# Gathers of a product-key layer: V half fetched apart from U, later, and only for weights that are not zero, in five of eight buffer slots

## The chip, the cores and the metric

The kernel runs on one core of one Trainium2 chip, as one program. The metric is the time of one execution on the device in microseconds. The kernel before took a median of 1542.22 us over the runs shown (1538.51 to 1542.54).

## The reference, cut to what matters

Two transformer blocks on 256 tokens of width 1024 are computed one after the other, all in float32. The change lies in the last layer of the second, a feed-forward layer with product keys (PEER). For each token and each of 8 heads it picks 16 of 16384 experts, which makes 128 experts a token:

```python
idx = jnp.take_along_axis(cand_idx, pos, axis=-1)     # 128 tokens x 8 heads x 16
g = jax.nn.softmax(best, axis=-1)
u = expert_u[idx]
v = expert_v[idx]
act = jax.nn.gelu(jnp.einsum('td,thkd->thk', xt, u))
return jnp.einsum('thk,thkd->td', (g * act).astype(xt.dtype), v)
```

`expert_u` and `expert_v` are tables of 16384 rows of 1024 floats (4 KB a row). The gain in front of the layer is large (`norm2_g_2` is drawn near 1 and multiplied by 44.634), so the dot products `xt . u` are tens in size, of both signs.

## The kernel before, in words

The first block, the attention and the recurrence of the second fill the program up to about 880 us; during it GpSimd also copies the two tables into one in HBM, `expert_uv`, whose rows are U beside V, 8 KB.

The last stage takes the experts in **rows**: row `i = 16 n + k` is the k-th expert of group n for each of 128 tokens (one token a partition). There are 16 groups (2 blocks of 128 tokens x 8 heads), so 256 rows. One row is handled in these steps, each on its own engine, with semaphores between them:

- GpSimd (L583 to L604): an indirect DMA gathers `expert_uv[idx]` into a buffer slot, 128 partitions x 2048 floats. There are 9 slots (`UV`, `SLOTS = 9`), and row i waits until TensorE has weighed row i-9 (`row_used`).
- VectorE (`row_dot`, L2399): the product of the U half with `H2N`, the token's vector in PSUM, summed to `dot`. Behind the dot of row k it issues one piece of the top-k of group n+2 (`top_part`), and at one row of a group the softmax's factor (`probabilities`).
- ScalarE (`weight`, L1611): gelu of the dot (`gel`), times the softmax's probability (`wts`), then a copy of the identity scaled by it (`DIAG`, 128 x 128). Once a group it computes the exponentials (`exp_best`), which needs another function table, loaded before and after.
- TensorE (`weigh`, L1163, and the loop in `weigh_rows`, L1199): the diagonal times the V half is added to the sum of the token block in PSUM, two matmuls of 512 columns. A float32 matmul stands in the trace as two records, so a row is four.

Each engine takes the rows in order. In groups 0 to 4 TensorE also makes two query chunks behind rows 2 and 6 of a group and the scores of a later group behind row 8; ScalarE drains them from PSUM in its own order of rows. Everything is issued in the order that the code is written in; the waits alone decide the times.

## Time and profile before

| | |
|---|---|
| Median of the runs shown | 1542.22 us |
| The profiled execution's own time | 1537.5 us |
| Its span in the trace | 1535.7 us |
| TensorE, VectorE, ScalarE, GpSimd busy | 92%, 75%, 52%, 22% |
| Software DMA queue (GpSimd's) | 432.01 MB, 72.4% of the engines' span |
| Mean of all DMA | 377 GB/s, and 421 to 422 in the last stage |

The span runs from the first to the last instruction in the trace. The shares are means over stages that differ; the last stage, some 640 of the 1536 us, is the one that the change touches, and is read by itself.

### The profile page before, as it was taken

How to read it: one execution, taken by the hardware profiler on the slowest of the kernel's cores; microseconds unless marked ns; L12 is line 12 of the kernel's file. 1: busy time of each engine (PE TensorE's matmuls, PEld its weight loads, DVE VectorE, ACT ScalarE, POOL GpSimd, SP SyncE). 2: the span in 40 equal slices, each digit the busy share in tenths (PEclk: the TensorE clock that was granted, in tenths of full speed). 3: DMA queues.
4: the chain of work that ended last, by engine and by line, in shares of the span. 5: the costliest groups of instructions: out<-in, count | busy, mean ns of one | idle time of the engine just before them, and what ended most of it. 6: DMA issues, size and time to landing. Idle time of an engine off the chain costs nothing.

```text
span 1535.7 us, 23394 instructions
## 1 busy us (share of the span) xinstructions
PE 1408.6 (92%) x7668; PEld 1025.0 (67%) x7668; DVE 1145.8 (75%) x2470; ACT 793.2 (52%) x1804; POOL 343.4 (22%) x445
## 2 busy tenths in 40 slices
PE   9999999999999999999999899999788787778777
PEld 8898899898888999998989864544232332222222
DVE  6667988887769988787897696666666667666644
ACT  6656544456666444476964434444444444444433
POOL 1111011111110111111110133443333333333331
PEclk9999999999999999999999999999999999999999
DMA  9999799999998999999999499999999999999996
GB/s 355 355 333 340 278 407 404 387 393 344 357 335 312 398 393 404 388 373 337 359 337 341 151 412 402 421 422 420 422 421 421 421 422 422 421 422 422 421 422 266
DMA packets 119267, 578.21 MB, mean 377 GB/s; under 512 B 11472, under 2 KB 11616, under 8 KB 85904
## 3 DMA queue, kind: packets, MB, share of 16 engines
q0 software_dynamic: 79584, 432.01, 72.4%
q1 hardware_dynamic: 39168, 142.97, 24.6%
q10 hardware_dynamic: 432, 2.19, 0.4%
q8 instruction: 44, 0.72, 0.2%
q14 instruction: 39, 0.32, 0.1%
HBM read 576.08 MB, written 135.27 MB: 463 GB/s over the span
## 4 chain that ended last, share of the span: by engine, by line
PE 47%; DMA 19%; DVE 7%; ACT 7%; issue 3%; POOL 0%; POOLq 0%; ACTq 0%; DVEq 0%
DMA late<-expert_uv,idx 11%; PE PS L1211 8%; PE PS L1171 8%; PE PS L672 5%; DMA attn<-expert_uv,idx 4%; PE PS L661 3%; PE PS L652 3%; PE PS L657 3%; DMA ada<-w_ada 3%; PE PS L678 2%; PE PS L1134 2%; ACT wrg L1623 2%; PE PS L701 1%; PE PS L803 1%; PE PS L917 1%
## 5 line engine op out<-in xcount | busy, mean ns | idle before, releaser
L1277 ACT ACTIVATE early_splits<-ring 128x1024 fp32r<-128x1024 f32 x166 | 175.3, 1056 | 89.2 <-PE PS L672 72.4
L1698 DVE TENSOR_TENSOR early_splits<-ring,early_splits 128x1024 fp32r<-128x1024 f32 x166 | 202.5, 1221 | 24.3 <-ACT early_splits L1277 23.9
L2403 DVE CUSTOM_DVE_ANT_0 attn<-attn,PS 128x1024 f32<-128x1024 f32 x115 | 140.4, 1221 | 91.4 <-DMA attn<-expert_uv,idx 90.1
L2403 DVE CUSTOM_DVE_ANT_0 late<-late,PS 128x1024 f32<-128x1024 f32 x113 | 138.0, 1221 | 92.1 <-DMA late<-expert_uv,idx 91.0
L1615 ACT ACTIVATE gel<-dot 128x1 f32<-128x1 f32 x256 | 51.1, 200 | 254.8 <-DVE dot L2403 254.6
L599 POOL DMA_INDIRECT attn<-expert_uv,idx x115 | 108.5, 944 | 244.1 <-PE PS L1211 96.5
L1211 PE MATMUL PS<-attn,wrg 128*128 128x512 f32 x256 | 128.7, 633 | 32.2 <-ACT wrg L1623 32.2
L599 POOL DMA_INDIRECT late<-expert_uv,idx x113 | 106.7, 944 | 178.4 <-PE PS L1211 93.3
L1211 PEld LDWEIGHTS PS<-attn,wrg 128*128 128x128 f32 x256 | 45.8, 195 | 113.7 <-ACT wrg L1623 70.6
L1211 PE MATMUL PS<-late,wrg 128*128 128x512 f32 x192 | 95.9, 623 | 26.0 <-ACT wrg L1623 25.9
L1171 PE MATMUL PS<-attn,wrg 128*128 128x512 f32 x204 | 98.3, 611 | 13.7 <-ACT wrg L1623 12.3
L1623 ACT ACTIVATE wrg<-con,wts 128x128 f32<-128x128 f32 x228 | 91.5, 401 | 21.7 <-PE PS L1211 0.8
L917 PE MATMUL PS<-product_split,early_splits 128*128 128x256 f32 x344 | 96.7, 281 | 1.9 <-DVE early_splits L1698 1.9
L921 PE MATMUL PS<-product_split,early_splits 128*128 128x256 f32 x344 | 97.3, 283 | 0.0
L922 PE MATMUL PS<-product_split,early_splits 128*128 128x256 f32 x344 | 97.2, 282 | 0.0
L1277 ACT ACTIVATE late_split<-ring 128x1024 fp32r<-128x1024 f32 x65 | 68.6, 1056 | 45.0 <-PE PS L672 33.2
L1211 PEld LDWEIGHTS PS<-late,wrg 128*128 128x128 f32 x192 | 33.3, 191 | 87.7 <-ACT wrg L1623 58.2
L1698 DVE TENSOR_TENSOR late_split<-ring,late_split 128x1024 fp32r<-128x1024 f32 x65 | 79.2, 1218 | 6.9 <-ACT late_split L1277 6.8
L672 PE MATMUL PS<-attn_split,late_split 128*128 128x512 f32 x320 | 82.0, 397 | 0.9 <-DVE attn_split L1704 0.9
L672 PE MATMUL PS<-attn_split,early_splits 128*128 128x512 f32 x320 | 80.7, 393 | 1.0 <-DVE attn_split L1704 1.0
L1171 PEld LDWEIGHTS PS<-attn,wrg 128*128 128x128 f32 x204 | 36.7, 192 | 66.2 <-issue 66.0
L1619 ACT ACTIVATE wts<-gel,prob 128x1 f32<-128x1 f32 x256 | 75.4, 295 | 9.3
(431 smaller groups left out, 3140.2 us busy)
## 6 DMA issues: line engine op xcount, KB each, us to landing
ring<-wstream SPq DMA_DIRECT2D x258, 512.0 KB, 9.0
expert_uv<-expert_u POOLq DMA_DIRECT2D x64, 1024.0 KB, 13.9
expert_uv<-expert_v POOLq DMA_DIRECT2D x64, 1024.0 KB, 15.6
ada<-w_ada POOLq DMA_DIRECT2D x32, 512.0 KB, 10.2
late<-w_ada POOLq DMA_DIRECT2D x16, 512.0 KB, 13.7
late<-wstream SPq DMA_DIRECT2D x4, 512.0 KB, 8.7
attn<-expert_uv,idx POOLq DMA_INDIRECT x115
late<-expert_uv,idx POOLq DMA_INDIRECT x113
```

The source lines that it names most:

```text
L599: gp.indirect_dma_start(UV[i % SLOTS], None, expert_uv, bass.IndirectOffsetOnAxis(ap=idx[:, n % 3, k:k + 1], axis=0)).then_inc(row_landed[ ...
L672: mm = pe.matmul(PS[:, bank, :].rearrange("p (s t) -> p s t", s=2), hi_of(u)[:, k * P:(k + 1) * P], x[:, :, k, :], start=(k == 0), stop=(k ...
L917: mm = pe.matmul(out_o, whi, FH[:, par, :], start=first and o % 2 == 0, stop=False, skip_group_check=True)
L921: pe.matmul(out_o, wlo, FH[:, par, :], start=False, stop=False, skip_group_check=True)
L922: mm = pe.matmul(out_o, whi, FL[:, par, :], start=False, stop=last, skip_group_check=True)
L1171: mm = pe.matmul(PS[:, 2 * b + g, :], DIAG[i % SLOTS], UV[i % SLOTS][:, D + g * 512:D + (g + 1) * 512], start=n % 8 == 0 and k == 0, stop= ...
L1211: mm = pe.matmul(PS[:, 2 * (first // (8 * EXPK)) + g, :], DIAG[m], UV[m][:, D + g * 512:D + (g + 1) * 512], start=False, stop=False, skip_ ...
L1277: act.activation(hi_of(u), raw(u), ACT.Copy).then_inc(hi_ready, 1)
L1619: act.activation(wts[:, s:s + 1], gel[:, s:s + 1], ACT.Copy, scale=prob[:, n % 2, k:k + 1]).then_inc(w_ready, 1)
L1623: act.activation(DIAG[i % SLOTS], ident, ACT.Copy, scale=wts[:, s:s + 1]).then_inc(diag_ready, 1)
L1698: ve.tensor_tensor(lo_of(u), raw(u), hi_of(u).bitcast(F32), ALU.subtract).then_inc(units_begun, 1)
L2403: ve.tensor_tensor_reduce(row, row, H2N[n // 8], 1.0, 0.0, ALU.mult, ALU.add, dot[:, n % 2, k:k + 1]).then_inc(dot_ready, 1)
```

## The change

- There are 8 slots instead of 9; the one that lay over the constants is gone. `DIAG` lies in `wrg` alone.
- In slots 1, 4 and 7 (`JOINT`) a row is fetched as before, U and V together, and weighed in its turn.
- In slots 0, 2, 3, 5 and 6 a row's U half is gathered from `expert_u`, as soon as the dot of the row eight before it is done. Its V half is gathered from `expert_v` by an instruction of its own, which GpSimd issues behind the U of the row six later (`V_LAG`).
- The index of V (`idx_v`) is made by VectorE in the row's own step (`pick_row`), by two small instructions: where the weight is exactly 0, 2^20 is added to the index. The gather has a bounds check at 16383 that lets such an index pass without a transfer; what the slot held stays there and is weighed by 0.
- ScalarE writes the diagonal of such a row seven steps later, and TensorE weighs it at the position of the row eight later. The last five of them are weighed behind row 255.
- The first wait of `probabilities` is on `w_ready` instead of `diag_ready`. The table `expert_uv` is still made in full.

```diff
-SLOTS = 9
+SLOTS = 8
+JOINT = (1, 4, 7)
+V_LAG = 6
+NO_ROW = float(1 << 20)
...
-                if i >= SLOTS:
-                    gp.wait_ge(row_used, i - SLOTS + 1)
-                gp.indirect_dma_start(UV[i % SLOTS], None, expert_uv,
-                                      bass.IndirectOffsetOnAxis(ap=idx[:, n % 3, k:k + 1], axis=0)
-                                      ).then_inc(row_landed[i % SLOTS], 16)
-
-            for i in range(ROWS):
-                row(i)
+                s = i % SLOTS
+                at = bass.IndirectOffsetOnAxis(ap=idx[:, n % 3, k:k + 1], axis=0)
+                if s in JOINT:
+                    if i >= SLOTS:
+                        gp.wait_ge(row_used, weighed_by[i - SLOTS])
+                    gp.indirect_dma_start(UV[s], None, expert_uv, at).then_inc(row_landed[s], 16)
+                else:
+                    if i >= SLOTS:
+                        gp.wait_ge(dot_ready, i - SLOTS + 1)
+                    gp.indirect_dma_start(UV[s][:, 0:D], None, expert_u, at).then_inc(row_landed[s], 16)
+
+            def row_v(i):
+                s = i % SLOTS
+                if s in JOINT:
+                    return
+                gp.wait_ge(rows_picked, separate(i + 1))
+                if i >= SLOTS:
+                    gp.wait_ge(row_used, weighed_by[i - SLOTS])
+                gp.indirect_dma_start(UV[s][:, D:2 * D], None, expert_v,
+                                      bass.IndirectOffsetOnAxis(ap=idx_v[:, s:s + 1], axis=0),
+                                      bounds_check=NKEYS * NKEYS - 1, oob_is_err=False).then_inc(v_landed[s], 16)
+
+            for i in range(ROWS + V_LAG):
+                if i < ROWS:
+                    row(i)
+                if i >= V_LAG:
+                    row_v(i - V_LAG)
...
             def weigh(i):
-                n, k = i // EXPK, i % EXPK
-                b = n // 8
-                pe.wait_ge(row_landed[i % SLOTS], 16 * (i // SLOTS + 1))
-                pe.wait_ge(diag_ready, i + 1)
+                r = i if joint(i) else i - SLOTS
+                if not 0 <= r < ROWS:
+                    return
+                b = r // (ROWS // 2)
+                pe.wait_ge(v_landed[r % SLOTS], 16 * (r // SLOTS + 1))
+                pe.wait_ge(diag_ready, spread_by[r])
...
                 act.activation(wts[:, s:s + 1], gel[:, s:s + 1], ACT.Copy, scale=prob[:, n % 2, k:k + 1]).then_inc(w_ready, 1)
-                if i >= SLOTS:
-                    act.wait_ge(row_used, i - SLOTS + 1)
-                act.wait_ge(w_ready, i + 1)
-                act.activation(DIAG[i % SLOTS], ident, ACT.Copy, scale=wts[:, s:s + 1]).then_inc(diag_ready, 1)
+                if joint(i):
+                    spread_weight(i)
+                if i + 1 >= SLOTS and not joint(i + 1):
+                    spread_weight(i + 1 - SLOTS)
...
+            def pick_row(i):
+                n, k, s = i // EXPK, i % EXPK, i % SLOTS
+                if s in JOINT:
+                    return
+                ve.wait_ge(w_ready, i + 1)
+                ve.tensor_scalar(no_row[:, s:s + 1], wts[:, s:s + 1], 0.0, NO_ROW, ALU.is_equal,
+                                 ALU.mult).then_inc(tokens_marked, 1)
+                if i >= SLOTS:
+                    ve.wait_ge(v_landed[s], 16 * (i // SLOTS))
+                ve.wait_ge(tokens_marked, separate(i + 1))
+                ve.tensor_tensor(idx_v[:, s:s + 1], no_row[:, s:s + 1], idx[:, n % 3, k:k + 1],
+                                 ALU.add).then_inc(rows_picked, 1)
...
                     if k == (4 if n else 14) and n + 1 < GROUPS:
                         probabilities(n + 1)
+                    pick_row(n * EXPK + k)
```

How the instructions stand on GpSimd late in the stage, before (`attn`, `late` and `con` are the tiles in which the slots lie, `idx` the indices; `x3` is three alike):

```order
L599 DMA attn<-expert_uv,idx 128x2048 [waits row_used] x3
L599 DMA late<-expert_uv,idx 128x2048 [waits row_used] x2
L599 DMA con<-expert_uv,idx 128x2048 [waits row_used]
L599 DMA attn<-expert_uv,idx 128x2048 [waits row_used,idx_ready]
L599 DMA late<-expert_uv,idx 128x2048 [waits row_used] x2
L599 DMA attn<-expert_uv,idx 128x2048 [waits row_used] x3
L599 DMA late<-expert_uv,idx 128x2048 [waits row_used] x2
L599 DMA con<-expert_uv,idx 128x2048 [waits row_used]
```

And now, for about six rows at the same place:

```order
L647 DMA attn<-expert_v,idx_v 128x1024 [waits row_used,rows_picked]
L633 DMA late<-expert_uv,idx 128x2048 [waits row_used]
L637 DMA attn<-expert_u,idx 128x1024 [waits dot_ready]
L647 DMA attn<-expert_v,idx_v 128x1024 [waits row_used,rows_picked]
L633 DMA attn<-expert_uv,idx 128x2048 [waits row_used]
L647 DMA late<-expert_v,idx_v 128x1024 [waits row_used,rows_picked]
L637 DMA attn<-expert_u,idx 128x1024 [waits dot_ready]
L637 DMA late<-expert_u,idx 128x1024 [waits dot_ready]
L647 DMA attn<-expert_v,idx_v 128x1024 [waits row_used,rows_picked]
```

Thirteen gathers stand where eight stood, each V behind the U or the joint gather of a row six later, and waits for VectorE (`rows_picked`, `dot_ready`) stand beside the one for TensorE.

VectorE in a group of the second half, before (`ISA` with `PS` is the dot, the `ISA` behind it reads its result; the rest is the top-k):

```order
L2403 ISA late,dot<-late,PS 128x1024 [waits row_landed4]
L2403 ISA dot 128x1
L2330 MAX best<-SQ 128x8 [waits topk_step]
L2403 ISA con,dot<-con,PS 128x1024 [waits row_landed5]
L2403 ISA dot 128x1
L2333 MATCH_REPLACE SQ<-best,SQ 128x256 [waits topk_step]
L2334 MAX_INDEX pk_i<-best,SQ 128x8
L2403 ISA attn,dot<-attn,PS 128x1024 [waits row_landed6]
```

And now, at the same pieces of the top-k:

```order
L2464 ISA late,dot<-late,PS 128x1024 [waits row_landed6]
L2464 ISA dot 128x1
L2391 MAX best<-SQ 128x8 [waits topk_step]
L2473 TENSOR_SCALAR no_row<-wts 128x1 [waits w_ready]
L2478 TENSOR_TENSOR idx_v<-no_row,idx 128x1 [waits tokens_marked,v_landed6]
L2464 ISA late,dot<-late,PS 128x1024 [waits row_landed7]
L2464 ISA dot 128x1
L2394 MATCH_REPLACE SQ<-best,SQ 128x256 [waits topk_step]
L2395 MAX_INDEX pk_i<-best,SQ 128x8
L2464 ISA attn,dot<-attn,PS 128x1024 [waits row_landed0]
L2464 ISA dot 128x1
L2398 MAX best<-SQ 128x8 [waits topk_step]
```

The two instructions of `pick_row` stand between a separate row's piece of the top-k and the next dot, and the first of them waits for the weight that ScalarE makes from the dot just before.

## Rows read from the trace of the kernel before

**Rows 1.** Page of the profile, its span and the traffic in 40 slices.
```profile
span 1535.7 us, 23394 instructions
...
GB/s 355 355 333 340 278 407 404 387 393 344 357 335 312 398 393 404 388 373 337 359 337 341 151 412 402 421 422 420 422 421 421 421 422 422 421 422 422 421 422 266
```

**Rows 2.** Busy time of each engine in a stretch of the gathers.
```profile
core 0: us, PE busy (x) PEld busy (x) DVE busy (x) ACT busy (x) POOL busy (x), PEclk, DMA share, GB/s
1300.00:1340.00 40.00, 31.46 (x66) 10.96 (x64) 27.49 (x75) 17.26 (x53) 15.03 (x16) 1.00 1.01 422
```

**Rows 3.** Timeline of VectorE: index casts behind rows 79 and 223, last dot.
```profile
1084.76 0.27 DVE L2374 CAST idx<-SQ 128x16 uint32<-128x16 f32 x1
...
1448.66 0.17 DVE L2374 CAST idx<-SQ 128x16 uint32<-128x16 f32 x1
...
1526.95 1.22 DVE L2403 CUSTOM_DVE_ANT_0 late<-late,PS 128x1024 f32<-128x1024 f32 x1 [1.23 <-DMA late<-expert_uv,idx]
```

**Rows 4.** Timeline of TensorE: row matmuls (L1171) and queries (L1134), groups 1 to 4.
```profile
940.31 3.62 PE L1134 MATMUL PS<-XN,MEM 128*128 128x256 f32 x16
...
982.48 5.31 PE L1171 MATMUL PS<-attn,wrg 128*128 128x512 f32 x12
987.63 3.62 PE L1134 MATMUL PS<-XN,ring 128*128 128x256 f32 x16
...
1054.53 3.62 PE L1134 MATMUL PS<-XN,ring 128*128 128x256 f32 x16
```

**Rows 5.** Timeline of one row's turn, all engines: start, length, what.
```profile
1301.45 1.22 DVE L2403 CUSTOM_DVE_ANT_0 late<-late,PS 128x1024 f32<-128x1024 f32 x1 [0.31 <-DMA late<-expert_uv,idx]
...
1302.59 0.08 DVE L2403 DVE_READ_ACCUMULATOR2_ANT dot<- 128x1 f32 x1
...
1302.71 0.20 ACT L1615 ACTIVATE gel<-dot 128x1 f32<-128x1 f32 x1 [1.46 <-DVE dot L2403]
...
1302.95 0.29 ACT L1619 ACTIVATE wts<-gel,prob 128x1 f32<-128x1 f32 x1
...
1303.33 0.40 ACT L1623 ACTIVATE wrg<-con,wts 128x128 f32<-128x128 f32 x1
...
1303.57 0.94 POOL L599 DMA_INDIRECT attn<-expert_uv,idx  x1 [1.55 <-PE PS L1211]
...
1303.79 1.98 PE L1211 MATMUL PS<-late,wrg 128*128 128x512 f32 x4 [0.50 <-ACT wrg L1623]
```

**Rows 6.** Busy time of each engine in a stretch of weight loads and table copies.
```profile
500.00:540.00 40.00, 40.00 (x269) 36.87 (x268) 35.73 (x56) 19.05 (x24) 6.00 (x11) 1.00 1.02 401
```

**Rows 7.** Timeline of GpSimd's first gathers, and the gathers' issues by tile `idx`.
```profile
883.60 0.94 POOL L599 DMA_INDIRECT attn<-expert_uv,idx  x1 [0.30 <-issue]
884.85 0.94 POOL L599 DMA_INDIRECT late<-expert_uv,idx  x1 [0.30 <-issue]
...
L599 POOL DMA_INDIRECT late<-expert_uv,idx x113: 937/939/1267, 879.5 to 1509.3; - x113
```

**Rows 8.** Timeline of VectorE: small instructions with a dot behind them, a top-k piece.
```profile
886.47 0.17 DVE L2371 SCALAR_TENSOR_TENSOR SQ<-SQ 128x8 f32<-128x8 f32 x1
886.67 0.17 DVE L2374 CAST idx<-SQ 128x8 uint32<-128x8 f32 x1
886.75 1.21 DVE L2403 CUSTOM_DVE_ANT_0 attn<-attn,PS 128x1024 f32<-128x1024 f32 x1
...
937.95 0.29 DVE L2396 TENSOR_SCALAR prob<-gexp 128x16 f32<-128x16 f32 x1
938.33 1.22 DVE L2403 CUSTOM_DVE_ANT_0 late<-late,PS 128x1024 f32<-128x1024 f32 x1
...
1365.70 0.68 DVE L2367 TENSOR_REDUCE SQ<-SQ 128x32 f32<-128x512 f32 x1
```

**Rows 9.** Timeline of ScalarE: first table load of a softmax to the next gelu.
```profile
1318.67 1.28 ACT L1608 ACT_TABLE_LOAD   x1
...
1321.67 0.20 ACT L1615 ACTIVATE gel<-dot 128x1 f32<-128x1 f32 x1
```

More of the change, by code:

```diff
@@ L389, in two_blocks @@
         row_landed = [sem(f"row_landed{k}") for k in range(SLOTS)]
+        v_landed = [row_landed[k] if k in JOINT else sem(f"v_landed{k}") for k in range(SLOTS)]
+        tokens_marked, rows_picked = sem("tokens_marked"), sem("rows_picked")
         h2_ready = sem("h2_ready")
@@ L467, in halves, with separate, joint, orders @@
             return PS[:, bank, :].rearrange("p (s t) -> p s t", s=2)[:, :, 0:nk]
+        def separate(rows):
+            return rows // SLOTS * (SLOTS - len(JOINT)) + sum(k not in JOINT for k in range(rows % SLOTS))
+        def joint(i):
+            return i % SLOTS in JOINT
+        def orders():
+            weighed, spread = {}, {}
+            for i in range(ROWS + SLOTS):
+                r = i if joint(i) else i - SLOTS
+                if 0 <= r < ROWS:
+                    weighed[r] = len(weighed) + 1
+                for r in (i, i + 1 - SLOTS):
+                    if 0 <= r < ROWS and joint(r) == (r == i):
+                        spread[r] = len(spread) + 1
+            return weighed, spread
+        weighed_by, spread_by = orders()
+        first_weighed = [min(range(b * ROWS // 2, (b + 1) * ROWS // 2), key=weighed_by.get) for b in range(2)]
+        last_weighed = [max(range(b * ROWS // 2, (b + 1) * ROWS // 2), key=weighed_by.get) for b in range(2)]
         block = ctx.enter_context(nc.Block())
@@ L1226, in _ @@
             natural_h2(1)
-            weigh_rows(6 * EXPK, 8 * EXPK - 1)
-            weigh(8 * EXPK - 1)
+            weigh_rows(6 * EXPK, 8 * EXPK - SLOTS)
+            for i in range(8 * EXPK - SLOTS, 8 * EXPK):
+                weigh(i)
             for k in range(EXPK):
@@ L1242, in _ @@
                     mm.then_inc(tile_for["act"], handed(4 + g, "act"))
-            weigh_rows(9 * EXPK, ROWS - 1)
-            weigh(ROWS - 1)
+            weigh_rows(9 * EXPK, ROWS - SLOTS)
+            for i in range(ROWS - SLOTS, ROWS + SLOTS):
+                weigh(i)
         @block.scalar
@@ L1666, in _ @@
                         exp_best(n + 2)
+            for i in range(ROWS + 1 - SLOTS, ROWS):
+                if not joint(i):
+                    spread_weight(i)
         @block.vector
```

43 lines of the change are left out of this document (23 added, 20 removed).

## The prediction

> **What bounds the kernel now.** First the stretches. In the last stage (row gathers, from about 890 us to the end) the DMA engines are busy without a gap and move 422 GB/s, while VectorE works 27.5 of 40 us, TensorE 31.5, ScalarE 17.3 and GpSimd 15.0 [rows 1, 2]. A gather of 128 rows of 8 KB is 1.0486 MB, so at 422 GB/s one takes 2.485 us, and that is the pace: the index casts of groups 4 and 13, nine groups of 16 rows apart, start 363.9 us apart, 2.527 us a row; from the dot of row 79 (1083.6, its cast less 1.15) to the last dot, at 1526.95, it is 443.3 us for 176 rows, 2.52 a row [rows 3]. The stage is bound by bytes. Groups 1 to 4 are different: there TensorE also makes queries and scores. Four records of one row take 1.72 us back to back (twelve in 5.15), a query 3.6, the scores about 1 [rows 4], so a group needs 16 x 1.72 + 7.2 + 1 = 35.8 us of TensorE; the queries at 940.31 and 1054.53, three groups apart, show 38.1 a group, against 39.8 for the bytes (16 x 2.485). Bytes and TensorE are almost level there.
>
> Then one turn, from the timeline [rows 5]. Times from the start of the dot: result read 1.14, gelu 1.26, weight 1.50 to 1.79, diagonal 1.88, matmul 2.34 to 4.32. VectorE does its piece of the next top-k behind the read.
>
> **What goes.** In slots 0, 2, 3, 5, 6 the V half of a row is fetched only where the weight is not zero. The trace cannot say how many are. The reference, evaluated on the inputs it draws, can: the dots have a standard deviation of about 46, gelu is exactly 0 below about -5, and 54.0% of the weights of these slots are nonzero. In half-rows of 4 KB per partition a round of eight rows costs 3 x 2 + 5 x 1.54 = 13.7 instead of 16 (half of them are V). Pace of the bytes: 13.7/16 x 2.485 = 2.13 us. Three additions. The groups with a top-k run 0.04 slower than the bytes alone (2.527 against 2.485), kept: 2.17. The skipped partitions fall unevenly on the sixteen DMA engines; if each serves eight partitions, whichever they are, the fullest has over a token block some 1.5% more than the mean by the reference's weights: 2.20. And 4 KB pieces may be dearer than 8 KB ones: a stretch that streams and copies 4 KB rows with the engines equally full moved 401 GB/s [rows 6]. That 5% on the 56% of bytes that are now in 4 KB pieces would make 2.26. Bounds of the byte pace: 2.13 and 2.26.
>
> **What is added on GpSimd.** 160 gathers: 13 issues in a round for 8. An issue takes 0.94 and the next follows 1.25 after it when nothing holds it [rows 7]; a half row is as many pieces (128) as a whole one, so I take the same price: 13/8 x 1.25 = 2.03 us a row. It hides behind the bytes, with 0.17 us to spare. The bounds check and the skipping are in no row. Bounds: 0.94 and 1.27, the longest of the gathers' issues in the trace [rows 7]; with 1.27 + 0.31 all through it is 2.57 a row, above the pace of before. I take 1.25, since the median is 0.939 and the minimum 0.937. Queued behind V of row i-6 is U of row i+1. V of row r waits for its index (about 2.2 after the start of dot r) and for TensorE to have passed position r (about 4 after it, by the chain of rows 5 and one more turn of 1.7); U of r+7 is wanted 7 turns, 15 us, after dot r, so about 10 us of transfers stay queued. The gather queue should not run dry.
>
> A rule of the Trainium skill speaks against this part. The row first: with VectorE at work in most of every window the issue stayed at a median of 0.939, and one was 1.27 [rows 2, 7]. The skill's page "SBUF — State Buffer", section "Who interferes with whom", says that GpSimd shares an SBUF port pair with VectorE, and that certain copies and tensor-scalar forms of VectorE shut GpSimd out while it writes descriptors. By the median the 160 added gathers cost nothing; by the rule, with the new small VectorE instructions, they could each come nearer 1.27. This is rival C.
>
> **What is added on VectorE.** 320 small instructions, two in a separate row's own turn, the first behind the row's weight. Nothing may start past them, the next dot above all. The weight ends 1.79 after the dot's start; I let the first start at 1.85. A dependent small instruction follows 0.20 behind its forerunner and a dot 0.08 behind that; in another place the dot came 0.38 after a small instruction [rows 8]. The pair costs between 0.28 and 0.76 (twice 0.38). I take 0.35, nearer the low end because there the dot had landed and nothing else stood between. A separate turn is then at least 2.20, in which the top-k piece is hidden unless it is longer than 0.7. A joint turn stays at VectorE's own work: 27.49 us for 16 rows [rows 2], 1.72, with gaps 1.87. A group: 8 x 2.20; one of 2.45, where the piece of 0.68 and what follows it is the longer arm [rows 8]; one of 2.86 behind the softmax, since its two table loads hold ScalarE for 3.0 us [rows 9] and row 12, a joint one, absorbs all but 0.65; and 6 x 1.87. Sum 34.1, or 2.13 a row. So VectorE comes level with the bytes; with the dear pair (0.76) it is 38.2, 2.39 a row.
>
> **Groups 1 to 4.** Before, VectorE ran ahead with dots while ScalarE stood waiting to drain a query bank. Now the index of a separate row waits for that row's weight, which stands behind the drain, so VectorE is tied to TensorE's position. Walking one group row by row with the durations of [rows 4, 5, 9], TensorE's 35.8 us get 2.5 of waiting for the diagonal of row 12 (late by the table loads) and about 1 for those of rows 15 and 1: 39.2 against 38.1. Three groups: +3 us. The bytes saved here buy nothing.
>
> **The end.** A separate row is weighed at the position of the row eight later, so five rows are left when the last diagonal comes: 5 x 1.72 = 8.6 us more behind the last dot, which before stood 8.75 us ahead of the end of the span [rows 1, 3]. The same five are missing in group 0; there VectorE's top-k pieces hold the row, so I give nothing back. ScalarE's later diagonals are as many as before and hidden: 0.3 each with over 20 us idle in a window of 40.
>
> **The sum.** The dot of row 79 started at 1083.6; now 1086.6. For the 176 rows after it I take 2.22, just above the two paces of 2.20 and 2.13 because a wait of either is not always covered by the other: 390.7. Last dot at 1477.3, end of span 1477.3 + 8.75 + 8.6 = 1494.7, against 1535.7: -41. The profiled execution took 1537.5 (1.8 around its span) and would take 1496.5; the runs shown have a median of 1542.2, 4.7 above it, so the forecast for the median is 1501.
>
> **Rivals.** A is the forecast, rate 2.17 to 2.28: 1492 to 1512. Chance 0.62.
>
> B: the weight's wait on VectorE takes the place of the bytes. With the pair at 0.76, 2.39 a row: 176 x 2.39 = 420.6, end 1524.6, time 1531. It cancels the gain at 2.44 a row, a pair of 0.84. For it: every separate turn now contains a round trip to ScalarE, and the earliest V transfer into the index's slot must have landed too. Against: ScalarE idles over half of each window. Chance 0.12.
>
> C, slower: GpSimd becomes the bound. At 1.58 an issue, 2.57 a row: 452 us, end 1556, time 1562. It decides from 2.44/1.625 = 1.50 an issue, 0.25 above the 1.25 shown. For it: the bounds check is in no row, and one issue did take 1.27; against: the even issue times. Chance 0.08. (The Trainium skill's page "SBUF — State Buffer", cited above, would have the issues drift that way.)
>
> D, slower: the change does not do what it says. If ScalarE's gelu leaves tiny values instead of zeros, or a skipped index still costs its transfer, the bytes are those of before: 2.52 a row, 443.5, end 1547.4, time 1554. Between, each tenth of V rows more adds 0.1 x 5/8 x 1.24 = 0.08 a row, 14 us; the gain is gone near nine tenths. For it: no row shows a weight. Chance 0.08.
>
> F: the early groups gain after all. If TensorE keeps the five rows' start and loses nothing to ScalarE, -8.6 instead of +3, and 2.17 after: end about 1476 to 1478, time 1484. For it: TensorE was nearly level there. Chance 0.10.
>
> **Numbers.** Predicted 1501. Own range of A 1492 to 1512; the range for 8 in 10 takes in F and most of B: 1484 to 1540. A measurement of this kernel can tell about 0.3% (4.6 us) from no change. Faster: A, F and seven of B's twelve, 0.79. Same: 0.05. Slower: C and D, 0.16.
>
> **What would show it.** In the profile after: gathers' bytes lower by 38 MB (160 x 0.46 x 0.524) and the rate still near 420 or VectorE's dots waiting for weights, not data; issues on GpSimd at 0.94; two small VectorE instructions 1.85 behind a dot's start and the next dot at 2.2; casts of groups 4 and 13 some 320 us apart (9 x 35.5) for 363.9; queries of groups 1 to 4 still 38 to 39 apart; five rows of matmuls back to back at the end. An unchanged byte count would prove D; issues of 1.2 and more back to back C; a dot-to-dot time of 2.6 in separate rows B.

## The result: no gain, a little slower

The changed kernel takes 1548.86 us (median of 20 runs, 1542.23 to 1556.38) against 1539.84 for the one before (20 runs, 1537.85 to 1546.22), a ratio of 1.0062 with a 95% interval of 1.0047 to 1.0077. The forecast was 1501, with a chance of 0.79 for faster and a range for 8 in 10 of 1484 to 1540; the measured time lies above it. The profiled execution has a span of 1542.8 us, where the sum of the prediction came to 1494.7.

The page of the changed kernel, with the lines that answer to [rows 1] and those on GpSimd and the packets:

```profile
span 1542.8 us, 24370 instructions
...
PE 1396.0 (90%) x7668; PEld 1040.5 (67%) x7668; DVE 1180.9 (77%) x2790; ACT 777.8 (50%) x1804; POOL 503.3 (33%) x605
...
GB/s 348 348 343 336 272 404 405 396 397 348 355 336 304 399 398 402 377 365 334 348 330 345 146 299 309 355 360 358 350 373 382 371 331 371 374 379 392 375 380 241
DMA packets 142315, 541.46 MB, mean 351 GB/s; under 512 B 23032, under 2 KB 23176, under 8 KB 129424
```

The bytes fell as forecast, from 578.21 to 541.46 MB, by 36.75 (38 were forecast), but with them fell the rate: 350 to 392 GB/s in the slices from about 1000 us on, once 331, where [rows 1] show 422. The line of the kernel before for the packets:

```profile
DMA packets 119267, 578.21 MB, mean 377 GB/s; under 512 B 11472, under 2 KB 11616, under 8 KB 85904
```

Two stretches of the changed kernel by busy time, the first to be laid beside [rows 2]:

```profile
core 0: us, PE busy (x) PEld busy (x) DVE busy (x) ACT busy (x) POOL busy (x), PEclk, DMA share, GB/s
1300.00:1340.00 40.00, 33.17 (x72) 13.74 (x71) 30.34 (x96) 16.60 (x54) 26.22 (x27) 0.96 0.98 374
1100.00:1500.00 400.00, 316.77 (x695) 130.09 (x693) 298.65 (x897) 165.85 (x538) 257.61 (x267) 0.97 0.98 374
```

No engine is full; GpSimd, the one that grew, is busy 26 of 40 us. Nor does the DMA share of 0.98 say that the transfers are: at a full rate they moved 422 GB/s before, and in the run without V gathers, below, the share reads 0.96 at 367. But GpSimd's 267 gathers in 400 us are one in 1.50 us, which becomes the clue below. VectorE's casts behind rows 31, 79 and 223 and its last dot, to be laid beside [rows 3] (the cast behind row 31 in the kernel before comes last):

```profile
977.70 0.17 DVE L2435 CAST idx<-SQ 128x16 uint32<-128x16 f32 x1
...
1101.84 0.17 DVE L2435 CAST idx<-SQ 128x16 uint32<-128x16 f32 x1
...
1450.99 0.35 DVE L2435 CAST idx<-SQ 128x16 uint32<-128x16 f32 x1
...
1525.47 1.22 DVE L2464 CUSTOM_DVE_ANT_0 late<-late,PS 128x1024 f32<-128x1024 f32 x1 [0.73 <-DMA late<-expert_uv,idx]
```

```profile
964.27 0.17 DVE L2374 CAST idx<-SQ 128x16 uint32<-128x16 f32 x1
```

So row 79 is 17.1 us later than before (1101.84 against 1084.76). From the dot of row 79 (1100.69, the cast less 1.15) to the last dot it takes 424.8 us for 176 rows, 2.41 a row: quicker than the 2.52 of before, far from the 2.22 of the forecast. From the last dot to the end of the span it is 17.33 us; the forecast had 17.35. The difference to the forecast sum, 48.1 us, is 34.1 of pace and 14.1 of start (row 79 was put at 1086.6).

### The profile page after: what moved, and what is told of

Its sections match the earlier page's. It is cut to its first block, busy times and chain, and to the rows that moved or that the text cites. A ratio compares the mean times of both kernels' runs of the same rounds, so it can differ in the third digit from the quotient of the medians.

```text
span 1542.8 us, 24370 instructions
## 1 busy us (share of the span) xinstructions
PE 1396.0 (90%) x7668; PEld 1040.5 (67%) x7668; DVE 1180.9 (77%) x2790; ACT 777.8 (50%) x1804; POOL 503.3 (33%) x605
## 2 busy tenths in 40 slices
DMA packets 142315, 541.46 MB, mean 351 GB/s; under 512 B 23032, under 2 KB 23176, under 8 KB 129424
## 3 DMA queue, kind: packets, MB, share of 16 engines
q0 software_dynamic: 102624, 395.19, 70.2%
q10 hardware_dynamic: 432, 2.19, 0.4%
## 4 chain that ended last, share of the span: by engine, by line
PE 50%; DVE 16%; issue 10%; DMA 10%; ACT 8%; POOL 5%; another core or an unknown queue 2%; POOLq 0%; DVEq 0%; ACTq 0%
PE PS L723 6%; DMA ada<-w_ada 6%; PE PS L1225 6%; PE PS L712 4%; PE PS L703 4%; PE PS L708 4%; PE PS L729 3%; PE PS L1262 3%; DVE late L2464 3%; PE PS L854 3%; PE PS L752 2%; DVE attn L2464 2%; DMA attn<-expert_u,idx 2%; DMA late<-expert_uv,idx 2%
## 5 line engine op out<-in xcount | busy, mean ns | idle before, releaser
L1759 DVE TENSOR_TENSOR early_splits<-ring,early_splits 128x1024 fp32r<-128x1024 f32 x166 | 202.4, 1220 | 24.6 <-ACT early_splits L1328 24.2
L1262 PE MATMUL PS<-late,wrg 128*128 128x512 f32 x288 | 145.8, 634 | 57.9 <-issue 37.7
L2464 DVE CUSTOM_DVE_ANT_0 attn<-attn,PS 128x1024 f32<-128x1024 f32 x128 | 155.5, 1216 | 25.8 <-issue 9.2
L2464 DVE CUSTOM_DVE_ANT_0 late<-late,PS 128x1024 f32<-128x1024 f32 x128 | 156.2, 1221 | 23.5 <-issue 14.5
L1225 PE MATMUL PS<-late,wrg 128*128 128x512 f32 x224 | 111.8, 626 | 39.9 <-ACT wrg L1666 34.7
L1262 PEld LDWEIGHTS PS<-late,wrg 128*128 128x128 f32 x288 | 53.6, 194 | 139.8 <-issue 110.6
L647 POOL DMA_INDIRECT attn<-expert_v,idx_v x96 | 96.5, 1005 | 122.6 <-PE PS L1225 38.7
L637 POOL DMA_INDIRECT attn<-expert_u,idx x96 | 90.1, 939 | 104.0 <-DVE idx L2435 74.8
L1262 PEld LDWEIGHTS PS<-attn,wrg 128*128 128x128 f32 x288 | 55.4, 197 | 90.4 <-issue 75.3
L1225 PEld LDWEIGHTS PS<-late,wrg 128*128 128x128 f32 x224 | 42.0, 196 | 96.5 <-issue 96.0
L576 POOL DMA_DIRECT2D expert_uv<-expert_v x49 | 26.9, 549 | 229.5 <-DMA expert_uv<-expert_u 217.4
L2473 DVE TENSOR_SCALAR no_row<-wts 128x1 f32<-128x1 f32 x160 | 24.4, 153 | 96.6 <-ACT wts L1677 54.4
L576 POOL DMA_DIRECT2D expert_uv<-expert_u x49 | 27.0, 550 | 188.9 <-DMA expert_uv<-expert_v 188.0
```

The lines of the kernel that those rows point to most:

```text
L637: gp.indirect_dma_start(UV[s][:, 0:D], None, expert_u, at).then_inc(row_landed[s], 16)
L647: gp.indirect_dma_start(UV[s][:, D:2 * D], None, expert_v, bass.IndirectOffsetOnAxis(ap=idx_v[:, s:s + 1], axis=0), bounds_check=NKEYS * N ...
L1225: mm = pe.matmul(PS[:, 2 * b + g, :], DIAG[:, r % 8, :], UV[r % SLOTS][:, D + g * 512:D + (g + 1) * 512], start=r == first_weighed[b], sto ...
L1262: mm = pe.matmul(PS[:, 2 * (first // (8 * EXPK)) + g, :], DIAG[:, m, :], UV[m][:, D + g * 512:D + (g + 1) * 512], start=False, stop=False, ...
L1759: ve.tensor_tensor(lo_of(u), raw(u), hi_of(u).bitcast(F32), ALU.subtract).then_inc(units_begun, 1)
L2464: ve.tensor_tensor_reduce(row, row, H2N[n // 8], 1.0, 0.0, ALU.mult, ALU.add, dot[:, n % 2, k:k + 1]).then_inc(dot_ready, 1)
```

## The experiments

"Pace" below is always the time from the dot of row 79 to the last dot over 176 rows, in the profiled execution. The kernels of gathers alone and of the small ring, and those with sixteen gathers, with thirteen in the kernel before and with four joint slots and all V skipped, have one execution each. Three theories stood at first: **D**, the transfers (a skipped partition costs time all the same, or 4 KB pieces are dear); **V**, VectorE's wait for the weight; **G**, GpSimd, its order of gathers at first, and from the second round on their number.

**Gathers alone.** A kernel that only gathers, in stretches: 8 KB rows, pairs, and the mix of the changed kernel, thirteen gathers in eight rows, with 46%, none and all of V skipped. Its core:

```
for i in range(80):
    gather 8 KB if i % 8 in JOINT else gather U (4 KB)
    r = i - 6
    if r >= 0 and r % 8 not in JOINT: gather V of r, bounds_check=16383
```

> This kernel computes nothing: it only issues gathers from GpSimd into buffer slots, eight deep and drained between sections, with index tables drawn at random, and writes zeros as output. Sections: (1) 48 gathers of 8 KB rows; (2) 32 pairs of an 8 KB gather and a 4 KB gather; (3) 32 pairs of an 8 KB gather and a bounds-checked 4 KB gather with every index out of bounds; (4) the same with 46% of the indices out of bounds; (5 to 7) ten rounds each of the kernel's own mix of 13 gathers for 8 rows, with 46%, none and all of the V indices out of bounds. Theory D (the transfers: a skipped partition still costs engine time, and a 4 KB piece costs more than half of an 8 KB one): 8 KB gathers 2.49 us apart; the pairs with all skipped at least 0.4 us above that, about 3.1; the mix with 46% skipped about 18.8 us a round (2.35 a row). Theory V or G (the transfers are as cheap as I counted, and the order of waits loses the time): pairs with all skipped no more than 0.1 above an 8 KB gather (or held at two issues, 2.55), the mix 17.0 to 17.4 us a round (2.13 to 2.17 a row).

Rows 32 to 72 of the three mixes came every 2.14 us with 46% skipped, 2.53 with none, 2.06 with all; 8 KB rows alone every 2.49. An 8 KB row beside an all-skipped gather came every 2.55: such a gather costs the transfers at most 0.06. The windows of the mixes with 46%, none and all skipped:

```profile
core 0: us, DVE busy (x) POOL busy (x), PEclk, DMA share, GB/s
...
500.00:640.00 140.00, 0.00 (x0) 103.72 (x108) 1.00 1.02 411
...
700.00:840.00 140.00, 0.00 (x0) 88.23 (x92) 1.00 1.02 414
...
920.00:960.00 40.00, 0.00 (x0) 30.24 (x33) 1.00 0.97 353
```

The transfers keep 411 GB/s, and the changed kernel's 0.898 MB a row would take 2.19 us. D falls, and the forecast's byte pace stands. With all skipped the pace is GpSimd's: 13 issues in 16.46 us, 1.27 each, without a pause.

**All of V read, none of V read.**

```diff
-NO_ROW = float(1 << 20)
+NO_ROW = 0.0                                   # all read
...
-... wts[:, s:s + 1], 0.0, NO_ROW, ALU.is_equal, ALU.mult)
+... wts[:, s:s + 1], 0.0, NO_ROW, ALU.mult, ALU.add)      # all skipped
```

> The changed kernel with 0 instead of 2^20 added to the index where the weight is zero, so that every V row is read. Its output is the same. Bytes as in the kernel before, 13 gathers a round. Theory D with about 0.6 us for a gather that is all skipped: skipping saves 0.625 x 0.46 x (1.28 - 0.6) = 0.2 us a row, so this runs some 35 to 50 us longer than the changed kernel, near 1590. Theory V (VectorE's turn is the bound, the transfers have slack): the pace goes only from 2.41 to the 2.49 of the bytes, +14 to +20 us, near 1565.

> The changed kernel with every V index of the five slots out of bounds: no V row is fetched there, and the matmuls weigh what the slot holds, so the output leaves those rows out. The instructions and waits are the same. Theory D: the transfers fall to about 2.1 us a row, and the pace to VectorE's 2.17: about 35 to 45 us faster than the changed kernel, near 1508. Theory V or G (waits of VectorE on the weight, or GpSimd's order): the pace stays at 2.35 to 2.41, 0 to 12 us faster, 1537 to 1549.

Reading all V (same instructions, the bytes of before): 1574.62 us, ratio 1.0213 (1.0189 to 1.0236), pace 2.57. Reading none of it in the five slots: 1549.02, ratio 1.0042 (1.0020 to 1.0065), pace 2.41, the same as with 46% skipped, at far fewer bytes. Its window:

```profile
1300.00:1340.00 40.00, 33.84 (x73) 14.02 (x73) 31.59 (x98) 17.64 (x58) 25.19 (x26) 0.96 0.85 298
```

So skipping does save 26 us against the same kernel that reads all; but the last bytes saved buy nothing, and the 2.41 isn't set by bytes.

**The index one step later.** In each step VectorE makes the index of the row before, whose weight has long come.

```diff
-                    pick_row(n * EXPK + k)
+                    if n or k:
+                        pick_row(n * EXPK + k - 1)
```

> The changed kernel with the index of V made one step later on VectorE (behind the next row's dot and its top-k piece), so that VectorE need not wait for ScalarE in the row's own turn; the rest as it is. Theory V: the 0.27 us a row that the first small instruction waited, and the 7 us in group 0, come back: 40 to 50 us faster than the changed kernel, near 1500. Theory D: only the start comes back, 5 to 12 us, near 1540.

1535.22 us, ratio 0.9961 (0.9944 to 0.9978). All of the gain lies ahead of row 79: from the first dot to that of row 79 it takes 199.2 us, against 213.5 in the changed kernel and 200.3 before. The pace doesn't fall: 2.44, where the changed kernel has 2.41. V holds for the start and falls for the rest.

**The number of gathers.** Four kernels, with 8, 12, 13 and 16 gathers in eight rows.

```diff
 # the changed kernel without its V gathers (V halves set to zero once)
                 if i >= SLOTS:
                     gp.wait_ge(row_used, weighed_by[i - SLOTS])
-                gp.indirect_dma_start(UV[s][:, D:2 * D], None, expert_v, ...)
...
 # four joint slots, with the later index
-JOINT = (1, 4, 7)
+JOINT = (1, 3, 5, 7)
...
 # the kernel before, with a second gather that moves nothing
                 row(i)
+                gp.indirect_dma_start(scrap[:, 2 * i:2 * i + 2], None, cells, <nowhere>, bounds_check=...)
```

> The changed kernel with the V gathers of the five separate slots left out: GpSimd waits for the index and for TensorE at their places as before, but issues nothing (V halves are set to zero once, and TensorE multiplies those). VectorE makes all indices, ScalarE all weights, in the same order. Eight issues in a round of eight rows instead of thirteen, and bytes of 1.71 us a row at the pace of the gathers alone. G (the number of gathers on GpSimd is the bound, 13 at 1.48 for eight rows = 2.41): the pace after row 79 falls to what VectorE's own walk needs, 2.13 to 2.2 a row, 40 us earlier than the 424.8 for 176 rows. V (round trip of the weight on VectorE): 2.4 a row stays, the span within 8 us of 1543.

> Slots 1, 3, 5 and 7 joint instead of 1, 4 and 7, and the index made one turn later, as in the run with the index one step later (span 1534.8, 2.435 a row after row 79). Twelve gathers in a round instead of thirteen; bytes of a round 4 x 2 + 4 x 1.54 = 14.2 sixteenths of 2.485 x 8, 2.20 a row. G: 12/8 x 1.48 = 2.22 a row, so 176 x 0.21 = 37 us off that run: last dot near 1480, span 1495 to 1500, and the ratio to the kernel before 0.972 to 0.978. V: the wait for the weight is already a turn behind, the pace of 2.43 is then VectorE's and ScalarE's chain, and one separate row less in eight changes it by at most a twentieth: span 1520 to 1535.

> The kernel before, with a second gather behind each of its 256: into 8 bytes of each partition of a spare tile, all indices out of bounds, so that it moves nothing and nobody waits for it. Sixteen issues in a round of eight rows. With an even issue of 1.27 a round takes 20.3 us, 2.53 a row: level with the 2.52 a row that the bytes set, span 1536 to 1545. G with its 1.48 for a gather: 2.96 a row, 110 us more over 256 rows, span near 1640. V expects the first.

> The kernel before with the second, all-skipped gather only behind rows of slots 0, 2, 3, 5 and 6: thirteen gathers in eight rows instead of sixteen (2.88 a row). G: 13/8 x 1.44 to 1.48 = 2.34 to 2.41 a row, less than the 2.52 that the bytes need, so the span stays at 1536 to 1545. If instead a skipped gather costs the transfers time (0.36 us each, by the run with sixteen: 2.88 less 2.52), the cost is added: 2.52 + 0.625 x 0.36 = 2.74 a row, span 1590.

Without V gathers, but with all their waits, indices and weights: pace 2.03, span 1465.3, ratio 0.953 (0.9491 to 0.957). Four joint slots: pace 2.31, 1508.82 us, ratio 0.9792 (0.9759 to 0.9825). Sixteen gathers, the eight more moving nothing and awaited by nobody: pace 2.88, 1640.52 us, 98 more than before. Thirteen of that kind: 2.56, span 1560.0, where the bytes alone want 2.49; neither no change nor the 2.74 of a cost to the transfers, so the two bounds add a little where they are close. Without V gathers VectorE makes every index behind its weight in its own turn, as in the changed kernel (only its and TensorE's waits for V to land are gone), at 2.03 a row: V is out. It also moves the same bytes as the run that reads none of V, which has its thirteen gathers and 2.41. G has it: 16 gathers at 2.88 are 1.44 each, 13 at 2.41 are 1.48.

The windows of the kernel without V gathers and of the one with sixteen:

```profile
1300.00:1340.00 40.00, 35.60 (x81) 14.57 (x80) 35.18 (x115) 19.04 (x63) 18.59 (x20) 1.00 0.96 367
```

```profile
1300.00:1340.00 40.00, 25.09 (x50) 10.59 (x51) 21.73 (x57) 16.12 (x49) 24.22 (x25) 0.83 0.87 325
```

GpSimd reads 24.2 of 40 where it is the bound: its busy time leaves out 0.30 behind each issue, and pauses. (TensorE's granted clock reads 0.83 in that window of the kernel with sixteen, but TensorE is busy only 25.1 of its 40 us.) The gathers of the changed kernel about one such pause, with GpSimd's timeline first, then TensorE's and VectorE's:

```profile
1313.01 1.00 POOL L647 DMA_INDIRECT late<-expert_v,idx_v  x1 [0.30 <-issue]
1314.32 0.94 POOL L637 DMA_INDIRECT attn<-expert_u,idx  x1 [0.31 <-issue]
1315.56 0.94 POOL L637 DMA_INDIRECT late<-expert_u,idx  x1 [0.30 <-issue]
1319.51 1.00 POOL L647 DMA_INDIRECT attn<-expert_v,idx_v  x1 [3.01 <-remote]
1320.81 0.94 POOL L633 DMA_INDIRECT late<-expert_uv,idx  x1 [0.30 <-issue]
...
1313.33 1.88 PE L1262 MATMUL PS<-attn,wrg 128*128 128x512 f32 x4
1315.04 1.88 PE L1262 MATMUL PS<-late,wrg 128*128 128x512 f32 x4
...
1315.72 0.15 DVE L2473 TENSOR_SCALAR no_row<-wts 128x1 f32<-128x1 f32 x1 [0.65 <-issue]
1317.33 0.16 DVE L2478 TENSOR_TENSOR idx_v<-no_row,idx 128x1 uint32<-128x1 f32 x1 [1.45 <-DVE no_row L2473]
```

The gather at 1319.51 is V of row 165. Its index was made at 1313.42, and TensorE's matmuls at that position, the upper of the two rows, ended at 1315.21, by their record; it could have gone at 1316.8. Between the dots of rows 79 and 240 GpSimd spends 57 us in gaps beyond the usual 0.30, 43 of them in 20 pauses for which index, dot and TensorE's matmul had all ended in time by their records. The 57 us are 0.36 a row: 2.06 and 0.36 make the 2.41.

But the wait was not met. The timeline puts the release down to `remote`, a semaphore event that no recorded end matches, and the semaphore events kept in the trace say which: TensorE's count `row_used` was raised at 1318.66 and again at 1318.73, and GpSimd's wait for it ended at 1318.69. The raise for a matmul that ended at 1315.21 came 3.5 us later, in one burst with the next. Of the 20 pauses 17 end so, within 0.03 us behind a raise of TensorE's count, up to 4.7 us after the matmul's end. TensorE's ends are modelled in these traces, so by its rows alone the matmul could have been late. VectorE's rows speak for late signals: its second small instruction follows the first by 0.26 us as a rule, here by 1.61, and it waited for nothing but the first one's own signal; in 5 of 145 turns the dot's result reached an idle ScalarE 0.4 to 2.1 us late, before in none of 152. Raises of TensorE's count more than 0.2 us behind its latest recorded end, between rows 79 and 240 and of those that the trace shows: none of 162 before, 37 of 97 in the changed kernel, 30 of 115 with all V skipped.

**Whose pauses are they?** Four kernels tried to bring them about, on the view that GpSimd's waits were met.

> It computes nothing of the reference. Five stretches of 80 rows, each with the mix of thirteen gathers in eight rows of the changed kernel, V six rows behind; in the first four all indices of V are out of bounds, in the fifth 46%. Beside them VectorE: (1) idle; (2) row dots from PSUM and SBUF, 128 x 1024, back to back; (3) pairs of 128 x 1 instructions of the kind that make the index; (4) a dot, a 128 x 256 product and a pair, in turn; (5) dots, as in 2. In the gathers alone, measured before, such rows came every 2.057 us (13 issues at a mean of 1.266) and 2.14 with 46% skipped. G, GpSimd as the bound by work of its own that VectorE's work makes dearer: in the changed kernel 13 gathers take 19.2 to 19.3 us over many turns, 1.48 each, in runs of even issues with one pause of 3 us; by that (1) is 2.06 and (2) or (4) near 2.4 a row, with such pauses. V, the weight's round trip: nothing here waits for VectorE, so all of 1 to 4 stay at 2.06 and 5 at 2.14. If all five stay, VectorE's port or load is not what makes a gather dearer in the kernel, and the 3 us pauses come from a wait in the kernel's own order.

> It computes nothing of the reference. Five stretches of 80 rows of gathers in the changed kernel's mix, V six rows behind. Alone, and beside VectorE's dots, such rows came every 2.07 us with all V skipped and 2.12 with 46% skipped (1.27 to 1.30 a gather), while inside the kernels a gather costs 1.44 to 1.48 on the average, because GpSimd pauses for 3 to 4 us every 13 to 34 gathers with its waits long met. Here: (1) beside matmuls of TensorE, all skipped; (2) beside ScalarE's 128 x 128 copies; (3) beside both and VectorE's dots; (4) as the kernels do it: no gather waits for a landing, each waits for the dot that freed its slot, V for its own row's dot, and VectorE waits for the landings; (5) as 4 with 46% skipped. If the pauses come from the load of another engine, 1, 2 or 3 goes to 2.3 to 2.4 a row with pauses of 3 us; if they come from the way in which gathers wait (a dot instead of a landing), 4 does; if from neither, all stay at 2.07 and 5 at 2.12 to 2.2, and the cause of the pauses stays open.

> It computes nothing of the reference. Four stretches of 80 rows of 8 KB gathers, each row waiting for the dot (1) or for TensorE's two matmuls (2 to 4) of the row eight earlier, VectorE's dot behind each landing; beside each row a second gather whose indices are all out of bounds (in 4 only in five rows of eight; in 3 of 8 bytes a partition and without any wait, as in the run where the kernel before has such a gather behind each of its own, 2.88 a row). Alone, such pairs came every 2.54 us, which is two even issues. In the kernels GpSimd pauses for 3 to 4 us with its waits long met, and each pause but one stands before a gather that waits for TensorE. If a wait for TensorE's semaphore is what makes the pauses, 1 stays at 2.54 to 2.6 and 2 and 3 go to 2.8 to 2.9; if not, all of 1 to 3 stay at 2.54 to 2.6 and 4 at 2.5.

> It computes nothing of the reference. Three stretches of 80 rows of 8 KB gathers, each with a skipped gather beside it (8 bytes a partition, no wait), VectorE's dot and TensorE's two matmuls on every row. In the ring run such rows came every 2.55 us where gathers waited for VectorE and TensorE had nothing to do, and every 2.81 and 2.88 where they waited for TensorE. Here TensorE works in all three; a gather waits (1) for SyncE, which waits for TensorE's semaphore and passes it on with an empty instruction; (2) for TensorE's semaphore itself; (3) for VectorE's dot, which stands behind TensorE here. If the pauses belong to the wait on TensorE's semaphore, 1 and 3 are at 2.54 to 2.6 and 2 at 2.8 to 2.9. If they belong to TensorE reading what gathers have written, all three are at 2.8 to 2.9.

Beside VectorE (dots; index pairs; both and a product) the all-skipped mix stayed at 2.072, 2.073 and 2.081, alone 2.072. Beside TensorE on tiles of its own, ScalarE, and all three: 2.072 each. With gathers that wait for dots, 2.072, and 2.23 with 46% skipped. None of these had a pause of 3 us, but in none of them did a gather wait for TensorE. Then a small model of the kernel's ring, where TensorE multiplies the gathered rows: pairs came every 2.55 without TensorE, 2.81 and 2.88 with it, with pauses of 3 to 8 us (thirteen gathers with TensorE: 2.44, where the 8 KB rows bind at 414 GB/s). The windows of its first three stretches:

```profile
core 0: us, PE busy (x) PEld busy (x) DVE busy (x) POOL busy (x), PEclk, DMA share, GB/s
100.00:240.00 140.00, 0.00 (x0) 0.00 (x0) 66.39 (x108) 106.47 (x111) 1.00 1.02 410
300.00:470.00 170.00, 120.14 (x235) 41.35 (x234) 72.54 (x118) 117.43 (x121) 0.97 0.97 371
540.00:700.00 160.00, 113.61 (x230) 38.61 (x228) 70.06 (x114) 110.70 (x114) 1.00 0.96 374
```

With SyncE passing TensorE's semaphore on, with the wait itself, and with VectorE behind TensorE, pairs came every 2.84, 2.86 and 2.89. That doesn't clear the wait: SyncE and VectorE waited for the same count of TensorE, and a raise that comes late holds them up as it holds GpSimd. Of the pauses of 2.5 us and more, all eleven in the ring's second and third stretch, 8 of 11 in these three and all eleven from 1122 to 1590 us in the kernel with sixteen gathers end within 0.3 us behind a raise of TensorE's count, most often in a burst (in the ring at 411.97, 412.03, 412.09 and 412.15, for matmuls that ended at 404.24 to 411.95, and the gather at 412.23). So the pauses need gathers that hang on TensorE's count and GpSimd without slack; what makes the raises late is open, and whether TensorE's work on gathered rows has a part in it as well, since no run has a gather wait for TensorE at work on other tiles. In the ring the time from issue to dot creeps up from 5.5 to about 8 us ahead of most of them and is back at 5.5 behind, while without TensorE it rose to 9.6 with no pause. A full queue alone doesn't explain that.

**Order, lag and slots.** With the later index throughout, except where said.

```diff
-JOINT = (1, 4, 7)
+JOINT = (1, 3, 4, 5, 7)        # five joint slots
...
+JOINT = (1, 3, 5, 7)           # four, with the index in the row's own step
...
+JOINT = (1, 3, 5, 7)           # four, V seven rows behind U
-V_LAG = 6
+V_LAG = 7
...
-V_LAG = 6                      # three, V seven rows behind U
+V_LAG = 7
```

> As the run with four joint slots (2.314 a row after row 79, span 1505.1), with five: slots 1, 3, 4, 5 and 7, the index a turn later. Eleven gathers in a round: 11/8 x 1.48 = 2.04 a row of GpSimd; bytes 0.958 MB a row, at 411 to 420 GB/s 2.28 to 2.33. G with the bytes as the next bound: 2.28 to 2.33 a row, so the span stays within 5 us of 1505, less 1.8 for one row fewer behind the last dot. If gathers alone set the pace, whatever the bytes, it falls by 11/12 to 2.12, and the span to 1470. V: no gain of its own.

> The changed kernel with slots 1, 3, 5 and 7 joint and nothing else: the index still in the row's own step. Of G, and of a start that the index in its own turn delays: the pace after row 79 as with the later index, 2.31 (2.22 to 2.35), and row 79 some 10 to 13 us later than there (1082.2), so a span of 1515 to 1520. V (the weight's round trip sets the pace of the later groups): 2.4 a row, span 1530 to 1540.

> The run with four joint slots and the later index, with V seven rows behind U instead of six. G: as many gathers, the same pace, span within 4 us of 1505. If part of the pace is GpSimd waiting at V for TensorE or the index, with U of later rows queued behind it, one row more of lag takes most of those waits away: 2.25 a row or less, span 1490 to 1495. Against that V lands a row later than TensorE's position for it; if that binds it gets slower by as much as 5 to 10 us.

> Slots 1, 4 and 7 joint as in the changed kernel, the index a turn later, V seven rows behind: the run of four joint slots with that lag (row 79 at 1075.5, 2.305 a row, span 1496.8) with thirteen gathers in a round instead of twelve and 3% fewer bytes. G (a gather costs GpSimd 1.48 on the average): 2.40 to 2.43 a row after row 79, span 1512 to 1522. If the order of waits is what costs, and GpSimd has time with the longer lag: 2.19 to 2.27 by the bytes, span 1480 to 1492.

> The run of four joint slots, later index and V seven rows behind (2.305 a row), with every V index of its four separate slots made out of bounds: V of those slots never fetched. Bytes fall from 0.928 to 0.786 MB a row, 1.9 us. If the bytes set the 2.305, the pace falls to 2.05 to 2.2 (GpSimd's twelve at 1.27 are 1.90, at 1.48 2.22), the span to 1460 to 1480. If GpSimd or the chain of waits sets it, it stays at 2.28 to 2.31, the span at 1495.

> The run with three joint slots, later index and V seven rows behind (2.393 a row after row 79, row 79 at 1093.3, span 1531.8), with one change: GpSimd waits for SyncE, which waits for TensorE's count and passes it on. Same thirteen gathers, same bytes. If the pauses of 3 us belong to GpSimd's wait on TensorE's semaphore, they go: GpSimd needs 13 x 1.27 / 8 = 2.06 and the bytes set the pace at 2.19 to 2.27, as the prediction had it: last dot near 1480, span 1490 to 1500, ratio 0.968 to 0.975. If they don't, nothing changes: 2.39, span 1532.

| gathers in 8 rows | kernel | pace | span | ratio to before |
|---|---|---|---|---|
| 11 | five joint, later index | 2.37 | 1510.1 | 0.9804 (0.9770 to 0.9838) |
| 12 | four joint, own step | 2.33 | 1530.1 | 0.9960 (0.9937 to 0.9982) |
| 12 | four joint, later index, lag 7 | 2.31 | 1496.8 | 0.9731 (0.9702 to 0.9760) |
| 12 | the same, all V of separate slots skipped | 2.22 | 1483.6 | |
| 13 | three joint, later index, lag 7 | 2.39 | 1531.8 | 0.9985 (0.9964 to 1.0006) |
| 13 | the same, SyncE passing TensorE's count on | 2.44 | 1537.2 | 0.9960 (0.9935 to 0.9984) |

Thirteen gathers give 2.39 to 2.44 in whatever order; twelve give 2.31 to 2.33, and 2.22, which is 12 x 1.48 / 8, once the bytes are out of the way. With five joint slots the bytes bind (0.958 MB in 2.37 us, 405 GB/s), and not one of 161 raises of TensorE's count is late there. The passed-on count changed nothing: SyncE gets it late too (68 of 111 raises by more than 0.2 us with the wait itself, 68 of 110 with it passed on). Four joint slots with the index in its own step end 25.0 us behind the same with the later index (1530.1 against the 1505.1 of the run above, both with lag 6); 21.9 of that is ahead of row 79, where 10 to 13 had been expected, so with four joint slots the own step costs more than with three (14.3).

The best, four joint with lag 7, has 1498.08 us (1497.27 to 1500.95): 41 less than before. The lag is worth 8.3 us of span, 6.8 of them ahead of row 79; no pace of 2.25 came of it. Its window and GpSimd's waits ahead of V gathers, from the view by tile:

```profile
1300.00:1340.00 40.00, 31.75 (x70) 12.37 (x69) 30.67 (x96) 18.13 (x58) 25.33 (x27) 1.00 1.01 401
```

```profile
its engine sat idle before it (us, times) until:
  DVE idx_v L2478: 73.2, 54
  issue: 26.5, 51
```

The transfers are full again (1.01 at 401 GB/s), and GpSimd has time to wait for the index in 54 places; pauses with all ends in time are down to 2 between rows 79 and 240, and none of 162 raises of TensorE's count is late.

## Why the prediction was wrong

**The step that failed** is the price of GpSimd: "13/8 x 1.25 = 2.03 us a row. It hides behind the bytes, with 0.17 us to spare." The 1.25 was the distance of two issues while GpSimd had slack; with thirteen in a round it has none, and then the mean price is 1.48, a round 19.3 us, 2.41 a row. The 0.21 us between an even issue of 1.27 and the 1.48 are, for the most part, waits for TensorE's count, which the prediction let pass "about 4 after" the dot and put at nothing ("The gather queue should not run dry"); by the semaphore events it came up to 4.7 us behind the matmul's end. That the number of gathers sets the pace is shown by count: 13, 12 (all skipped) and 16 gathers give 2.41, 2.22 and 2.88, with transfers and weights changed beside them without effect. Why the count comes late is not shown. The combined 2.22 a row rested on this step; it cost 34.1 us. Rival C named the mechanism, with "1.50 an issue" as the point from which it decides, and the runs put it at 1.44 to 1.48, just short; C had it as a dearer issue, while the issues stayed even (0.94 and 1.00) and waits between them made the price, so its sign, "issues of 1.2 and more back to back", never showed.

**The start** failed in one half. Groups 1 to 4 were right: groups 2 to 4 take 124.1 us by their casts (977.70 to 1101.84) against 120.5 before (964.27 to 1084.76), +3.6 where +3 was forecast. Wrong was "The same five are missing in group 0 ... so I give nothing back": by row 31 the changed kernel is 13.4 late. 3.8 of it stand ahead of the first gather (879.50 against 875.7), which no run explains. The rest is the index in its own step beside the query drains; VectorE and GpSimd in group 0:

```profile
891.99 0.15 DVE L2473 TENSOR_SCALAR no_row<-wts 128x1 f32<-128x1 f32 x1 [1.29 <-ACT wts L1677]
...
896.87 0.15 DVE L2473 TENSOR_SCALAR no_row<-wts 128x1 f32<-128x1 f32 x1 [1.85 <-ACT wts L1677]
...
893.14 1.00 POOL L647 DMA_INDIRECT attn<-expert_v,idx_v  x1 [4.82 <-DVE idx_v L2478]
...
911.21 1.00 POOL L647 DMA_INDIRECT attn<-expert_v,idx_v  x1 [6.39 <-DVE idx_v L2478]
```

The run with the later index took 14.3 us off ahead of row 79, 9.3 of them by row 31 (80.1 us from the first dot to that of row 31, for 89.4).

**What was right.** The bytes saved (36.75 of 38 MB) and their pace: 2.13 to 2.26 was given, and gathers alone need 2.14 to 2.19. A separate turn of VectorE: 2.20 given, 2.16 where nothing was late (dots at 1303.78 and 1305.94). The tail: 17.35 given, 17.33 measured. VectorE's 2.13 a row was an upper price: with no V gathers to wait for, the same instructions ran at 2.03. Rival B (the weight's wait) had nearly the measured pace, 2.39 a row, from the wrong cause: the later index took the wait away and the pace stayed. D was refuted by the byte count and by gathers alone; F by the start.

On the port that GpSimd shares with VectorE: thirteen gathers in a round beside VectorE's dots kept 2.072 a row, and beside dots, products and small instructions 2.081, with issues of 0.968 us for 0.963 on the average and 1.19 at most. The Trainium skill, page "SBUF — State Buffer", section "Who interferes with whom", lets some of VectorE's forms shut GpSimd out; by these runs that is worth 0.01 us a row here.

## What to carry over

An engine that only issues is full well before its busy time says so: count its instructions in a long stretch and divide, and take its price from a stretch in which it has no slack, or from a kernel that doubles them. Trading bytes for gathers pays only while both stay below the pace: here, with the later index, eleven and twelve gathers in eight rows did, thirteen hardly (0.9961 and 0.9985), and the best split was the one in which transfers and GpSimd needed the same time (four joint slots, 41 us faster than before). A wait that is put into an engine's own turn is paid where its source is busy with something else, so make the value one turn later. And before a wait is called met because its source had ended, look at when the semaphore was raised: here the two lay up to 4.7 us apart.

## What the runs showed of the hardware

- A gather whose partitions are all skipped is no cheaper to issue (1.00 us and 0.30 behind it, against 0.94 and 0.30), and each skipped partition is still a small packet: the packets of GpSimd's queue rose by 23040 (79584 to 102624), 144 for each of the 160 V gathers, and those under 512 B from 11472 to 23032. The Trainium skill, page "DMA: Bandwidth & Descriptors", section "The descriptor swizzle", counts 9 write descriptors on each of 16 engines for a 1 MiB transfer to 128 partitions; the 144 agree. The time that an all-skipped gather costs the transfers is at most 0.06 us.
- With GpSimd issuing gathers without slack, semaphores are raised late and in bursts: TensorE's count up to 4.7 us behind the recorded end of its matmul (37 of 97 raises by more than 0.2 us; with slack, in the kernel before and with four joint slots and lag 7, none of 162), and VectorE waits 1.61 us for its own signal where 0.26 is the rule. A gather that waits for such a count makes a pause of 3 to 4 us every 13 to 34 gathers (3 to 8 us in the small ring). Passing the count on through SyncE or VectorE doesn't take the pauses away; where no gather hangs on TensorE's count there are none. A full GpSimd alone doesn't bring the late signals: beside TensorE and ScalarE on tiles of their own all 1094 raises by VectorE and ScalarE came in time. Nor does it take TensorE: beside VectorE alone 241 of 991 raises by VectorE were late. The cause stays open.
- From the start of an 8 KB gather's issue to the dot on it takes 5.5 us at the least.
